# ScalarE's order inside a run of attention units: both first exponentials ahead of the copies of turned blocks

## What is computed

```
# mixer A: chunks of 64 queries, 8 earlier chunks and their own as keys, a bias by relative distance
sc = einsum('bqhd,bkhd->bhqk', qc, kc) * scale + bias
sc = where(valid, sc, NEG_INF)
p  = softmax(sc, axis=-1)
o  = einsum('bhqk,bkhd->bqhd', p, vc)
# mixer B: window of 2 chunks, 8 query heads on 2 key heads, rotary q and k, a learned sink per head
m = maximum(max(sc), sink)
p = exp(sc - m);  p = p / (sum(p) + exp(sink - m))
o = einsum('bnhgqk,bnkhd->bnqhgd', p, vb)
# around it
proj = rms_norm(x) @ w_in
x = x + (g_a * y_a + g_b * y_b) @ w_out
x = x + (silu(g_part) * u_part) @ w_down
```

## Time and profile before

| | |
|---|---|
| runs | 2611.38, 2609.62, 2613.55 us; median 2611.38 |
| profiled execution | 2611.81 us, its span 2610.0 us |
| granted TensorE clock, mean of the span | 0.997 of full speed |
| TensorE busy | 2574.6 us, 99% |
| VectorE busy | 1824.1 us, 70% |
| ScalarE busy | 1045.2 us, 40% |
| GpSimd busy | 285.3 us, 11% |

### The profile page before, as it was taken

How to read it: one execution, slowest core, us unless ns; L and a number is a source line. 1 busy time by engine, 2 the same in 40 slices (tenths; PEclk the granted TensorE clock), 3 DMA queues, 4 the chain that set the end, 5 groups by cost and what they waited for, 6 DMA issues and landing times. The chain is left out here.

```text
span 2610.0 us, 35611 instructions
## 1 busy us (share of the span) xinstructions
PE 2574.6 (99%) x12824; PEld 2096.9 (80%) x12824; DVE 1824.1 (70%) x3319; ACT 1045.2 (40%) x2071; POOL 285.3 (11%) x442
## 2 busy tenths in 40 slices
PE   8999999999999999999999999999999999999998
PEld 6888777788888888888788887777888888888886
DVE  8766555554888778768996665555458778776687
ACT  6222456532533333344542225664235333333444
POOL 0000322344000000000000012224430000000000
PEclk9999999999999999999999999999999999999999
DMA  4323543353132233395423244424422233235843
GB/s 153 123 105 125 164 136 114 123 178 128 57 117 101 89 113 122 97 279 161 150 105 121 101 147 148 141 83 162 161 105 85 90 113 121 81 105 162 261 117 125
DMA packets 201518, 337.47 MB, mean 129 GB/s; under 512 B 18817, under 2 KB 81153, under 8 KB 201345
## 3 DMA queue, kind: packets, MB, share of 16 engines
q1 hardware_dynamic: 193120, 312.00, 36.4%
q10 hardware_dynamic: 8224, 23.20, 2.6%
HBM read 241.28 MB, written 92.93 MB: 128 GB/s over the span
## 5 line engine op out<-in xcount | busy, mean ns | idle before, releaser
L1386 PE MATMUL ps<-op_hi,up_hi 128*128 128x512 f32 x1232 | 479.9, 389 | 2.5 <-DVE third_sum L2944 2.5
L1388 PE MATMUL ps<-op_hi,up_lo 128*128 128x512 f32 x1232 | 479.3, 389 | 0.0
L1387 PE MATMUL ps<-op_lo,up_hi 128*128 128x512 f32 x1232 | 479.3, 389 | 0.0
L1386 PE MATMUL ps<-in_hi,up_hi 128*128 128x512 f32 x728 | 285.9, 393 | 2.1 <-DVE up_lo L2450 2.1
L1387 PE MATMUL ps<-in_lo,up_hi 128*128 128x512 f32 x728 | 284.5, 391 | 0.0
L1388 PE MATMUL ps<-in_hi,up_lo 128*128 128x512 f32 x728 | 284.4, 391 | 0.0
L1386 PEld LDWEIGHTS ps<-op_hi,up_hi 128*128 128x128 f32 x1232 | 231.3, 188 | 50.8 <-issue 3.3
L1387 PEld LDWEIGHTS ps<-op_lo,up_hi 128*128 128x128 f32 x1232 | 231.3, 188 | 48.2
L1388 PEld LDWEIGHTS ps<-op_hi,up_lo 128*128 128x128 f32 x1232 | 231.3, 188 | 47.9
L2050 ACT ACTIVATE up_hi<-up_raw 128x512 fp32r<-128x512 f32 x252 | 158.0, 630 | 278.5 <-PE ps L1388 271.6
L1386 PE MATMUL ps<-act_hi,dn_hi 128*128 128x512 f32 x616 | 240.2, 390 | 1.2 <-DVE dn_lo L3119 1.2
(11 more groups left out here) (253 smaller groups left out, 4820.1 us busy)
## 6 DMA issues: line engine op xcount, KB each, us to landing
up_raw<-w_gu SPq DMA_DIRECT2D x42, 1024.0 KB, 5.2
act_raw<-ff_saved SPq DMA_DIRECT2D x154, 256.0 KB, 2.8
w_quarter<-w_lin SPq DMA_DIRECT2D x52, 512.0 KB, 4.5
w_raw<-w_lin SPq DMA_DIRECT2D x48, 512.0 KB, 4.2
ff_saved<-ff_block SPq DMA_DIRECT2D x88, 256.0 KB, 2.0
ff_saved<-ff_mix SPq DMA_DIRECT2D x66, 256.0 KB, 2.0
gated<-gates_saved SPq DMA_DIRECT2D x32, 512.0 KB, 4.2
dn<-w_dn_a SPq DMA_DIRECT2D x48, 256.0 KB, 4.0
```

The source lines that it names most:

```text
L1386: pe.matmul(out, w1, x1, start=first, stop=False, skip_group_check=True)
L1387: pe.matmul(out, w1, x0, start=False, stop=False, skip_group_check=True)
L1388: return pe.matmul(out, w0, x1, start=False, stop=last, skip_group_check=True)
```

## The change

In ScalarE's attention loop the copies of the turned blocks of the run before, and the value copies that start with the run, move from the run's first step (s equal to the start) to its second (start + 1), behind the exponential of that step. For s = 128, which has no unit, they stay where they were. The exponential of the sinks keeps its step, so it now stands ahead of the copies.

```
@@ -1942,10 +1942,10 @@
                                 take_values(L, c, part)
                     if s < UNITS:
                         soften(L, s)
-                    if s > 0 and s == run_start(s):
-                        take_turned(L, s - 1)
-                    if s == run_start(s):
-                        for c, part in turns_at(s):
+                    if s == UNITS or s == run_start(s) + 1:
+                        if run_start(s) > 0:
+                            take_turned(L, run_start(s) - 1)
+                        for c, part in turns_at(run_start(s)):
                             take_values(L, c, part)
                     if eight_at(s, EIGHT) is not None and unit(s - 1)[0] == "B":
                         soften_sinks(L, eight_at(s, EIGHT))
```

## The result

The changed kernel took 2621.32 us (median of 5 runs, 2620.22 to 2622.2), the kernel before 2611.2 us in 5 runs beside it. The ratio is 1.0036 with a 95% interval of 1.0025 to 1.0047, so it is 10.1 us slower (6.5 to 12.3). The profiled execution has a span of 2619.5 us against 2610.0.

The account below looks back on a forecast made before the run. The prediction took TensorE's instruction stream as the bound, busy 99% of the span. Four delays, 6.4 + 2.1 + 0.6 + 0.5 = 9.6 us, added to 2611.4 gave 2621.0 us, range 2616.0 to 2625.5.

Parts of the forecast that it names:

- a stretch from 500 to 1560 that changes length: Sign against the prediction: the kernel outside the attention stretches was to keep its length.
- (1): Seventh A run (p = 6) of every group: weighing 0.80 us later, eight times, 6.4 us.
- (2): Third A run (p = 2), groups 1 to 3: weighing 0.35 us later, 2.1 us; group 2 partly a run earlier.
- (3): Fifth A run (p = 4), groups 1 to 3: weighing 0.10 us later, six times, 0.6 us.
- (4): Last B run, groups 0 to 2: copy behind sink exponential and exponential b, weighing 0.09 us later, 0.5 us in all.
- The duration that decides: ScalarE: 0.83 us from a 640-column exponential to the next operation, by the trace; 0.72 by the skill page.
- (5): Other runs, such as the sixth A run: copies stay covered, no loss; a delay is not added to the next run.
- The gain: none.: Transposes behind exponential b: ending b earlier frees nobody; gain 0.
- A: Rival: TensorE regains part of the delay in waits for VectorE's row maximum; 2617.0 us, lower end 2616.6; chance 0.14.
- B: Rival: no difference, lost time made up elsewhere or the edit inert; 2611.4 to 2616.6 us; chance 0.08.
- C: Rival: faster, transposes wait for the exponential and their 11.0 us of idle goes; 2606.8 us; chance 0.02.
- D: Rival: worse, delays add as ScalarE's third copy pushes the next exponential a; 2623 to 2626 us; chance 0.08.

Follow-up runs that it names:

- experiment 4: Kernel before, with one gate step moved from the start of run p = 6 to the start of p = 7; 2612.52 us, ratio 1.0002.
- experiment 1: Kernel before, with the new order only in the eighth A run (p = 7) of each group; 2619.24 us against 2612.15, ratio 1.0028.
- experiment 2: Kernel before, with the new order in all runs but the eighth A run; 2614.66 us against 2612.15, ratio 1.001.
- experiment 3: Changed kernel, with one gate step moved from the start of run p = 6 to the start of p = 7; 2614.72 us, ratio to the kernel before 1.0014.
- experiment 7: Kernel before, with the new order only in the fifth A run (p = 4), delaying the fourth run's copies; 2612.5 us against 2611.81, ratio 1.0002.

## Why the prediction was right, point by point

**The bound.** Right: 99% TensorE with 4.0 us to spare over both stages meant that a wait put into its stream is paid in full. The rest of the kernel gave nothing back that can be told from the scatter between executions: the -0.92 us between the stages lies inside the -1.43 to +0.23 of the other kernels. The sign named for this, a stretch from 500 to 1560 that changes length, was too strict: in the kernel of experiment 4, which has the old order, it changes by -1.11.

**(1) to (4).** Right, each in place and size: 0.80 forecast and 0.79 measured at p = 6, 0.35 and 0.34 at p = 2, 0.10 and 0.11 (the mean) at p = 4, 0.09 and 0.08 in the last B runs; 9.6 together and 9.48 in the table. The split of (2) over two runs in group 2 did not come in the kernel after. The weighing starts 0.07 behind the end of the second copy (320.89 to 320.96), where I took 0.06. That these are sums of rows and not luck is shown by experiments 1 to 3.

**The duration that decides.** From exponential a to exponential b it is 319.02 - 318.19 = 0.83 us, the value taken from the earlier trace rows. The Trainium skill ("ScalarE: Activation LUTs", section "What ACT_TABLE_LOAD costs") gives, as an estimate by its formula, 0.72 for this shape, and by it the time would have been 2618.3. The measured step of 0.79 at p = 6 decides for 0.83; 0.72 would have made it 0.69.

**(5).** Right in kind: the sixth run stayed covered, and a delay relieves the next one (experiment 7). The remainders of 0.03 at p = 3 and p = 5, 0.39 in all, were forecast as nothing. One sentence of it is wrong: that the sixth run would cost what (1) costs if its gate step went. Experiments 3 and 4 take that step away. Compared with each other, their p = 5 steps differ by 0.00 in group 0 and by 0.03 in groups 1 to 3, the same as with the gate step in place, and not by 0.79: the last scores alone hide the copies there. By the prediction's own rows the cost could be no more than 0.17 us, 363.30 + 0.06 against 363.88 - 0.69 = 363.19.

**The step that failed: "The gain: none."** I looked for a gain only at exponential b, and there was none there. But the change moved a third thing, the exponential of the sinks, past the copies, and I priced it only as 0.10 on ScalarE's queue, in (4). Its reader is VectorE, with row maxima queued behind the waiting sum, and TensorE's scores wait for those. That was worth -1.50 us. Together with the remainders the shown sum is 8.4 and not 9.6; the median moved by 10.1, and the 1.7 between lies inside the interval. So the time 2621.0 against 2621.3 agrees better than its parts do, and that closeness is luck.

**The rivals.** A (regained): none of it at the places named, the gain of 1.5 came by another way. B, C and D did not come: not inside the noise, no gap of 0.17 vanished, and delays relieve each other. The time given for C was summed wrong: it says that (1) to (4) are still paid, which is 9.6 and not 6.4, so 2610.0. **The signs.** Two were told wrong: the profile puts the idle before the eight weighings down to "issue" and not to the copy L1931, and the stretches grew by 4.34 and 4.05 us, not 4.8.

## What to carry to other kernels

On an engine with slack, don't ask how busy it is, but for each result how long before its reader it ends. At p = 6 that was 0.08 us, of which 0.07 is what a weighing that waits for a copy L1931 shows anyway, and 0.79 of the 0.83 us of one activation put ahead was paid by the bound engine; one piece of the bound engine's own work put into the gap (0.69 us) hid all but 0.1. When a block of instructions is moved, follow every result of it, the smallest too: here eight columns held up VectorE and through it TensorE. When whole times scatter more than the terms, compare the starts of one repeated instruction in two traces, run by run.

## What the runs showed that I had not expected

The repeated steps agree between executions to about 0.02 us (0.79 eight times, and again eight times in another kernel), while the start of the first weighing moves by up to 3.04 us between executions whose input stage is the same code. The few steps that do not repeat, as 0.10, 0.40 and 0.55 at one place, go with a VectorE product of 0.69, 0.98 and 1.13 us in front of them. And a wait that holds TensorE for 0.8 us can stand in the profile without a name: "issue" before L1583.
